# Down projections of a feed-forward stage cut into three token pieces instead of two

## The reference, cut to what matters

```
def swiglu(h, w1, w3, w2):
    return (jax.nn.silu(h @ w1) * (h @ w3)) @ w2
...
        h = h + 0.5 * swiglu(rmsnorm(h, ffn2_norm[i]), ffn2_w1[i], ffn2_w3[i], ffn2_w2[i])
    return rmsnorm(h, final_norm)[:, N_META:]
```

## Time and profile before

| what | value |
|---|---|
| three executions, median | 3610.93 us |
| profiled execution, its own time | 3607.34 us |
| its span, first to last instruction | 3605.6 us |
| TensorE busy | 3520.8 us, 98% of the span |
| weight loads (PEld) busy | 2933.4 us, 81% |
| VectorE, ScalarE, GpSimd busy | 41%, 27%, 31% |
| mean granted TensorE clock | 0.991 of full speed |

### The profile page before, as it was taken

The page is one execution under the profiler, slowest core; times in us unless marked ns, Lnnn a source line. Parts: engine busy times, 40 slices in busy tenths (PEclk is TensorE's granted clock), DMA queues, the critical chain, the costliest instruction groups (busy, mean ns, idle before and its releaser), DMA issues.

```text
span 3605.6 us, 52857 instructions
## 1 busy us (share of the span) xinstructions
PE 3520.8 (98%) x20076; PEld 2933.4 (81%) x20076; DVE 1465.4 (41%) x2553; ACT 963.0 (27%) x1684; POOL 1132.6 (31%) x1499
## 2 busy tenths in 40 slices
PE   8999899999999999999999999999999999999998
PEld 6787778888888889899999878887777888888886
DVE  7865545211111263322122563737876521111214
ACT  5254533111111142110111332215663411111112
POOL 4433045222223252222222532300025532222323
PEclk9999899999999999999999999999999999999999
DMA  3113022111111121111111332110024311111113
GB/s 125 41 49 86 1 100 82 51 54 42 51 40 54 48 81 49 46 47 47 47 47 45 99 101 69 42 35 33 33 92 149 94 57 54 47 44 50 47 45 102
DMA packets 81556, 218.51 MB, mean 61 GB/s; under 512 B 18928, under 2 KB 19056, under 8 KB 80880
## 3 DMA queue, kind: packets, MB, share of 16 engines
q1 hardware_dynamic: 61792, 173.35, 15.5%
q10 hardware_dynamic: 19600, 42.88, 3.3%
HBM read 195.67 MB, written 19.46 MB: 60 GB/s over the span
## 4 chain that ended last, share of the span: by engine, by line
issue 61%; POOL 24%; PE 9%; DVE 4%; ACT 1%; POOLq 1%; DMA 0%; DVEq 0%; ACTq 0%; SPq 0%
POOL w_lo L572 24%; PE acc L731 2%; PE acc L732 2%; PE acc L733 2%; DVE cv_acc L1747 2%; PE acc L1281 0%; PE acc L1276 0%; POOLq L576 0%; PE acc L1398 0%; DVE ssq L680 0%; PE acc L1340 0%; PE acc L1415 0%; DVE tmp L692 0%; DVE cvo L1838 0%; PE acc L1407 0%
## 5 line engine op out<-in xcount | busy, mean ns | idle before, releaser
L572 POOL TENSOR_TENSOR w_lo<-w_raw,w_hi 128x256 fp32r<-128x256 f32 (+3 forms) x1480 | 1111.8, 782 | 2352.4 <-ACT w_hi L542 2351.9
L731 PE MATMUL acc<-h_hi,w_hi 128*128 128x512 f32 (+1 forms) x3520 | 1301.4, 370 | 15.8 <-issue 4.7
L732 PE MATMUL acc<-h_lo,w_hi 128*128 128x512 f32 (+1 forms) x3520 | 1300.8, 370 | 0.0
L733 PE MATMUL acc<-h_hi,w_lo 128*128 128x512 f32 (+1 forms) x3520 | 1295.7, 368 | 0.0
L731 PEld LDWEIGHTS acc<-h_hi,w_hi 128*128 128x128 f32 x3520 | 662.7, 188 | 143.2 <-issue 13.3
L732 PEld LDWEIGHTS acc<-h_lo,w_hi 128*128 128x128 f32 x3520 | 662.0, 188 | 118.3 <-issue 1.9
L733 PEld LDWEIGHTS acc<-h_hi,w_lo 128*128 128x128 f32 x3520 | 663.3, 188 | 114.9
L542 ACT CAST w_hi<-w_raw 128x1024 fp32r<-128x1024 f32 (+3 forms) x370 | 346.3, 936 | 1205.1 <-PE acc L733 1190.5
L1012 DVE TENSOR_TENSOR ff_hi<-tmp,acc 128x512 f32 (+3 forms) x154 | 94.6, 614 | 1098.6 <-PE acc L733 1066.6
L731 PE MATMUL acc<-ff_hi,w_hi 128*128 128x512 f32 (+1 forms) x1232 | 447.2, 363 | 6.1 <-POOL w_lo L572 3.4
L732 PE MATMUL acc<-ff_lo,w_hi 128*128 128x512 f32 (+1 forms) x1232 | 443.2, 360 | 0.0
(11 more groups left out here) (377 smaller groups left out, 3010.4 us busy)
## 6 DMA issues: line engine op xcount, KB each, us to landing
w_raw<-in_ffn_w_dram SPq DMA_DIRECT2D x94, 512.0 KB, 3.5
w_raw<-in_w_in_dram SPq DMA_DIRECT2D x60, 512.0 KB, 3.5
w_raw<-in_w_out_dram SPq DMA_DIRECT2D x32, 512.0 KB, 3.5
w_raw<-in_ffn_w_dram SPq DMA_DIRECT2D x48, 320.0 KB, 2.8
w_raw<-in_w_gate_dram SPq DMA_DIRECT2D x24, 512.0 KB, 3.5
w_raw<-in_w_up_dram SPq DMA_DIRECT2D x24, 512.0 KB, 3.5
w_raw<-in_ffn_w_dram SPq DMA_DIRECT2D x32, 384.0 KB, 3.0
gates_kept<-gstage ACTq DMA_DIRECT2D x32, 256.0 KB, 2.0
```

What stands on the lines that cost most here:

```text
L572: pool.tensor_tensor(w_lo[:, j, a:a + step], w_raw[:, j, a:a + step], w_hi[:, j, a:a + step].bitcast(F32), ALU.subtract).then_inc(split_do ...
L731: pe.matmul(bank, wh, rh, start=(k == 0), stop=False)
L732: pe.matmul(bank, wh, rl, start=False, stop=False)
L733: ins = pe.matmul(bank, wl, rh, start=False, stop=(k == seg.kt - 1))
```

## The change

The down segments of parts 0, 1 and 2 of the last feed-forward stage get token pieces of their own. All other segments keep theirs. The wait for `ff` before each piece of the first slab is worked out from how many of the two up chunks the piece reaches into.

```diff
 CH1 = [(META, 512), (META + 512, 512)]
 CH2 = [(0, 264), (264, 264), (528, 512)]
+PIECES = {("ffn2", 0): [(META, 320), (META + 320, 384), (META + 704, 320)],
+          ("ffn2", 1): [(META, 508), (META + 508, 508), (META + 1016, 8)],
+          ("ffn2", 2): [(META, 496), (META + 496, 496), (META + 992, 32)]}
...
             if part < len(FQ) - 1:
-                add(f"{name}_down{part}", KD // 2, nf, chunks, run(wd[part], 0))
+                add(f"{name}_down{part}", KD // 2, nf, PIECES.get((name, part), chunks), run(wd[part], 0))
...
                 down = SEG[f"{name}_down{part}"]
-                for c in range(len(chunks)):
-                    pe.wait_ge(sem("ff_" + name), part * len(chunks) + c + 1)
+                for c, (c0, w) in enumerate(down.chunks):
+                    whole = sum(a < c0 + w for a, _ in chunks)
+                    pe.wait_ge(sem("ff_" + name), part * len(chunks) + whole)
                     pe_slab(pe, down, 0, 0, (ff_hi, ff_lo), only=c)
```

## The result

The changed kernel took 3640.47 us (median of three runs, 3637.69 to 3643.50), against 3610.93 us before: a ratio of 1.0083, 95% interval 1.0060 to 1.0106. Slower by 29.5 us, where 28.6 us were forecast.

The account below looks back on a forecast made before the run. TensorE's own stream was taken to bound the kernel. Parts 0, 1 and 2 add 1.2 + 15.6 + 11.8 = 28.6 us to the 3610.9 us median: 3639.5 us, 0.79% slower, own range 3632 to 3645.

Parts of the forecast that it names:

- What bounds it: Down segments of the last stage's parts 0, 1, 2: TensorE's own stream sets the time, busy throughout at full clock.
- The price of a narrow matmul: Parts 1 and 2: 112 ns for 8 and 32 columns alike; net +15.6 us and +11.8 us.
- The Trainium skill's 81 ns: Its figure for a 128-column matmul in load and matmul pairs; would make the sum 8.2 us smaller, some 20 us.
- The price of width: Wide pieces of all three parts: a straight line from 120.6 ns at 264 columns to 226.6 ns at 512.
- The bound of 1.9 us for part 0: Upper bound on part 0's +1.2 us, if each matmul carries 13.3 ns over its columns at 2.4 GHz.
- The cover at the start of part 0: First piece's matmuls cover the second piece's wait for both hidden chunks; cover shrinks from 1.8 to 0.3 us, still holds.
- The median against the profiled execution: Whole kernel: the runs' median lies 3.6 us above the profiled execution; 3635.9 us profiled, 3639.5 us median.
- Everything before 2990 us: Profile after the change: everything ahead of the changed down segments stays unmoved.
- Two loads for a narrow product: Rival for narrow pieces: each done in two passes, 222 ns a product, 29.0 us on top, 3669 us; chance 0.07.
- Loads held ahead: Rival: several loads fetched ahead and held, narrow matmuls cost only their columns, change brings 1.2 us, 3612 us; chance 0.04.
- the Trainium skill's gap of some 25 ns: Its rule for matmuls of 1 to 64 columns; by it the sum would be about 6 us.
- The falling clock: Rival: each 8-column piece in part 1 brings 3.5 us at half speed, some 14 us, 3653 us; chance 0.08.

Follow-up runs that it names:

- The part kernels: Three kernels, each keeping the new pieces of one part only, against the kernel before: 3.0 us (part 0), 15.5 us (part 1), 11.8 us (part 2) more.
- The short load: The changed kernel with part 1's 8-column piece computed for 32 of 128 output features, so loads of 32 columns: 3629.73 us, 10.7 us less than the changed kernel.
- the longer series: The changed kernel timed again in more rounds (5 runs) beside the kernel before (15 runs): 3639.39 us, 31.0 us more, ratio 1.0088.
- the one with 27 narrow matmuls: The changed kernel with half of part 1's 8-column piece computed one time more, 27 matmuls in a row instead of 18: 3652.88 us.
- the one with 36: The changed kernel with part 1's 8-column piece computed twice over, 36 matmuls in a row instead of 18: 3670.85 us.
- the interleaved kernel: The changed kernel with k-steps outer and pieces inner in parts 1 and 2, save each part's first slab, so narrow matmuls stand between wide ones: 3640.42 us.

## Why the prediction was right, point by point

*What bounds it.* Right. TensorE's stream is the path: the part kernels add up, and TensorE waits for no other engine in the changed stages.

*The price of a narrow matmul, 112 ns for 8 as for 32 columns.* Right, to the nanosecond, from one-column matmuls of another type and stage. The short load shows why it could be carried over: the price is that of loading 128 columns of weights. The Trainium skill's 81 ns (TensorE: Matmul & The Clock Gate, Back-to-back issue gap) was set aside for the row's 112, and 128 columns took 112 here too.

*The price of width, 0.427 ns a column between 264 and 512.* This is the term that was mis-sized. Two ends don't make a line: 496 columns took 225 ns (219.8 by the line), 508 took 227 (224.9), 384 took 175 and 320 took 146.5 (171.8 and 144.5). The bound of 1.9 us for part 0 failed with it: it gave each matmul the 13.3 ns that a 512-column one has over its columns, and the 384-column ones have nearly 15, so the slabs say 2.1 us. By the slabs the line is the whole of the difference in each part: 8 x 18 x (2 x 2.0 + 3.2) ns = 1.0 us in part 0, 8 x 36 x 2.1 = 0.6 us in part 1, 8 x 30 x 5.2 = 1.2 us in part 2, together some 2.8 us, and 31.3 - 28.6 is 2.7. The measured 29.5 us hid this. That it came within 0.9 us of the forecast was luck: a sum 2.7 us too small met runs that differ by more than that, and the longer series has 31.0.

*The cover at the start of part 0.* Right: 0.3 us of it were forecast to be left. The last `ff_lo` ended at 2994.97 and the 384-column piece began at 2995.30, without a wait. With the narrow piece first the cover is gone and the stall is there.

*The median against the profiled execution.* The forecast put the 3.6 us between them on top, which suited the median; the profiled execution after was the median run itself, so against 3635.9 us it was 4.6 us higher, 2.7 of them the width and the rest in stages that the change doesn't touch. Everything before 2990 us was forecast to be unmoved, and that failed by 1.0 us: the first down matmul of part 0 starts at 2992.66 instead of 2991.70. The other 1.0 us lies behind part 2. Traces of kernels with the same code up to there differ by more: the first eviction of part 0 comes at 2995.65 in the changed kernel, at 2992.80 in the one with 27 narrow matmuls and at 2998.01 in the one with 36.

*Rivals.* Two loads for a narrow product: no, they would have been 222 ns apart. Loads held ahead: no, by the interleaved kernel; the Trainium skill's gap of some 25 ns for up to 64 columns (the same page, same section) isn't what a stream of full loads gave here, 112 ns at 64 columns; it was come near to only with a load of 32 columns (32 ns). The falling clock: not here, but it is real and its price was well estimated (1.6 us a fall, where 1.75 was estimated). A narrow run half as long again brought it in five slabs of eight. The rows cited against it, 1.8 us of one-column matmuls every 12.9 us at a clock of 1.00, said nothing of 2.0 us every 10.2, so that it stayed away was in part luck.

## What to carry to other kernels

Cutting a moving side of 512 columns into more pieces with the same stationary blocks costs a full set of weight loads. Here they lay hidden beneath pieces of 256 columns and more, where a further piece cost only the 11 to 20 ns that each matmul takes beyond its columns; a remainder of 8 columns cost as much as one of 128. If a remainder can't be avoided, make the pieces even (320, 384, 320 cost 0.26 us a slab, 508, 508, 8 cost 2.03), and don't put the small one where it has to cover a wait.

## What the runs showed of the hardware that had not been expected

- A TensorE that the profile shows as fully busy can still be followed by a lower clock. Runs of 8-column matmuls count as fully busy in the profile (3.80 of 3.80 us with 36 in a row), and yet the granted clock fell to the 1.2 GHz level after 4.0 us of them every time, after 3.0 us in five of eight slabs, and after 2.0 us never, unless TensorE then stood still as well (2.0 us of them and a stand of 0.34 us; 1.7 us of 32-column ones and a stand of 0.58 us).
- A matmul's fixed part beyond its columns isn't one number: 11 to 20 ns between 256 and 512 columns, and 4 ns more for 512 columns when the rows of the moving operand are 1040 columns apart instead of 1088. At 508 columns the longer row helped too (slabs of 10.19 against 10.27 us), at 320, 384 and 496 columns it didn't (8.42 against 8.38, 8.43 against 8.41). Why isn't shown. The up segments, whose rows are 1040 long, run at 231.7 ns. Whether longer rows there would bring them to 226.6 wasn't tried and isn't shown. If they did, 5 ns for each of some 8000 matmuls would be about 40 us (an estimate), more than the change costs. No version that beats the kernel before was run.
